# A PEER layer's dense expert products with 32 tokens taken out instead of 16, and GpSimd's share of the weight remainders laid out anew

## The reference, cut to what matters

```python
PEER_HEADS, PEER_NKEYS, PEER_TOPK = 8, 128, 16

def peer_ffn(h, w_pq, sub_keys, expert_u, expert_v):
    q = (h @ w_pq).reshape(B, S, PEER_HEADS, 2, PEER_DQ // 2)
    scores = jnp.einsum('bshpd,hpkd->bshpk', q, sub_keys)
    top_s, top_i = lax.top_k(scores, K)
    cand_s = top_s[..., 0, :, None] + top_s[..., 1, None, :]
    cand_i = top_i[..., 0, :, None] * NK + top_i[..., 1, None, :]
    best_s, best_pos = lax.top_k(cand_s.reshape(B, S, PEER_HEADS, K * K), K)
    expert_idx = jnp.take_along_axis(cand_i.reshape(B, S, PEER_HEADS, K * K), best_pos, axis=-1)
    gate = jax.nn.softmax(best_s, axis=-1)
    u = jnp.take(expert_u, expert_idx, axis=0)
    a = jnp.einsum('cd,chkd->chk', h, u)
    w = gate * jax.nn.gelu(a, approximate=False)
    return jnp.einsum('chk,chkd->cd', w, jnp.take(expert_v, expert_idx, axis=0))
```

## Time and profile before

| | |
|---|---|
| median of 3 runs | 2774.8 us (2772.82 to 2775.05) |
| profiled execution, its own time | 2772.15 us |
| its span, first to last instruction | 2770.4 us |
| PE busy | 2693.1 us, 97% of the span |
| DVE busy | 2127.9 us, 77% |
| ACT busy | 1381.1 us, 50% |
| POOL busy | 382.7 us, 14% |
| HBM | 206 GB/s over the span |

### The profile page before, as it was taken

One profiled execution on the slowest core, in us unless ns is written; L12 is line 12 of the kernel. 1 busy time (PEld: TensorE's weight loads), 2 busy tenths in 40 slices (PEclk: granted clock), 3 DMA queues, 4 the chain that ended last, 5 costly groups with the idle time before them and its releaser, 6 DMA issues.

```text
span 2770.4 us, 39894 instructions
## 1 busy us (share of the span) xinstructions
PE 2693.1 (97%) x16254; PEld 2321.3 (84%) x16254; DVE 2127.9 (77%) x3176; ACT 1381.1 (50%) x1632; POOL 382.7 (14%) x294
## 2 busy tenths in 40 slices
PE   7999999999999999999999999999999999999998
PEld 6778888788888888998888888897889988788887
DVE  7787887775555579989978777646699989888776
ACT  4645446554455455554444344464555554434443
POOL 0210002000023001122102012040011222002121
PEclk8999999999999999999999999999999999999999
DMA  8757876466553355555456588644555655456785
GB/s 312 268 198 296 313 257 225 155 213 197 190 199 129 135 190 191 205 198 170 166 183 212 185 290 295 225 150 139 165 180 197 209 182 176 149 198 218 258 289 185
DMA packets 86470, 574.34 MB, mean 207 GB/s; under 512 B 9840, under 2 KB 10352, under 8 KB 23056
## 3 DMA queue, kind: packets, MB, share of 16 engines
q1 hardware_dynamic: 75888, 534.86, 55.1%
q0 software_dynamic: 10400, 36.93, 3.8%
HBM read 563.32 MB, written 8.44 MB: 206 GB/s over the span
## 4 chain that ended last, share of the span: by engine, by line
PE 84%; DVE 8%; ACT 3%; issue 3%; DMA 1%; POOL 1%; SPq 0%; POOLq 0%; DVEq 0%; ACTq 0%
PE banks L492 22%; PE banks L499 11%; PE banks L590 11%; PE banks L592 10%; PE banks L600 10%; DVE wlo L1610 3%; PE banks L564 2%; PE banks L566 2%; PE banks L575 2%; ACT whi L1095 2%; PE banks L1030 2%; PE banks L534 1%; PE banks L536 1%; PE banks L546 1%; PE banks L630 1%
## 5 line engine op out<-in xcount | busy, mean ns | idle before, releaser
L1095 ACT ACTIVATE whi<-raw 128x2048 fp32r<-128x2048 f32 x438 | 839.7, 1917 | 962.6 <-issue 761.7
L1610 DVE TENSOR_TENSOR wlo<-raw,whi 128x2048 fp32r<-128x2048 f32 x422 | 977.0, 2315 | 240.6 <-ACT whi L1095 239.8
L492 PE MATMUL banks<-ht,whi 128*128 128x480 f32 (+1 forms) x2848 | 675.1, 387 | 5.9 <-DVE big L1708 3.4
L492 PEld LDWEIGHTS banks<-ht,whi 128*128 128x128 f32 x2848 | 524.0, 190 | 88.9 <-issue 3.6
L590 PE MATMUL banks<-whi,ht 128*128 128x512 f32 x1152 | 454.5, 395 | 10.4 <-DVE ht L1698 10.4
L592 PE MATMUL banks<-whi,ht 128*128 128x512 f32 x1152 | 449.8, 390 | 0.0
L499 PEld LDWEIGHTS banks<-ht,wlo 128*128 128x128 f32 x2848 | 351.7, 190 | 11.4
L499 PE MATMUL banks<-ht,wlo 128*128 128x240 f32 (+1 forms) x2848 | 354.0, 277 | 0.0
L600 PE MATMUL banks<-wlo,ht 128*128 128x512 f32 x1152 | 288.8, 390 | 2.1 <-DVE wlo L1610 2.1
L590 PEld LDWEIGHTS banks<-whi,ht 128*128 128x128 f32 x1152 | 216.9, 188 | 56.5 <-issue 12.1
L600 PEld LDWEIGHTS banks<-wlo,ht 128*128 128x128 f32 x1152 | 216.7, 188 | 47.9 <-DVE wlo L1610 3.0
(11 more groups left out here) (311 smaller groups left out, 3579.1 us busy)
## 6 DMA issues: line engine op xcount, KB each, us to landing
raw<-in_pu SPq DMA_DIRECT2D x128, 1024.0 KB, 4.9
raw<-in_pv SPq DMA_DIRECT2D x128, 1024.0 KB, 4.9
raw<-in_win SPq DMA_DIRECT2D x52, 1024.0 KB, 4.9
big<-in_wmod SPq DMA_DIRECT2D x28, 1024.0 KB, 7.1
raw<-in_wgate SPq DMA_DIRECT2D x22, 1024.0 KB, 6.4
raw<-in_wup SPq DMA_DIRECT2D x22, 1024.0 KB, 5.7
raw<-in_wdown SPq DMA_DIRECT2D x22, 1024.0 KB, 5.0
raw<-in_wmod SPq DMA_DIRECT2D x20, 1024.0 KB, 5.1
```

Of the source, the lines that this page charges most:

```text
L492: m = e.matmul(wide(b + n, t), h[:, q, c[n]], x[:, q], start=q == 0, stop=False, skip_group_check=True)
L1095: e.activation(whi(j), slot[u][0], ACT.Copy).then_inc(*hi.mark(j))
L1610: e.tensor_tensor(wlo(j), slot[u][0], whi(j).bitcast(F32), ALU.subtract).then_inc(*lo.mark(j))
```

## The change

Thirty-two tokens are left out instead of sixteen (NT 224, 28 groups, SUB 4, 32 dots and 32 additions a layer). In the first product POOL makes the remainders of 13 units (37, 39, ... 61) instead of 8, in the second those of 14 (1, 3, 5 and 10, 12, ... 30) instead of none. The list for the first has an entry for each head of the selection; all but the last are empty here. `pace` makes sets in odd units alone, two each and three in units 37, 49 and 61. The dots stand in units 9 to 34 and the additions in 37 to 61. The buffers of the tokens left out are laid out anew, two of the four row buffers, `HREP` and `ACC` behind the experts' results, and POOL's order in the second product is written unit by unit.

```diff
-FEW = 16
+FEW = 32
 NT = 256 - FEW
 SUB = P // FEW
 NG = NT // 8
 RINGS = 4
-POOLED = (37, 40, 43, 46, 49, 52, 55, 58)
+POOLED = (), (), (), (), (), (), (), (), tuple(range(37, 62, 2))
+POOLED_V = (1, 3, 5, *range(10, 31, 2))
...
-    OH = [[at(f"oh0{i}", 73728 + 4 * (29696 + 1024 * i), 2048, F16) for i in range(3)],
+    OH = [[at(f"oh0{i}", 73728 + 4 * (28672 + 1024 * i), 2048, F16) for i in range(3)],
...
-    HREP, ACC, ROWS_OF, PICK = 2048, 3072, 4096, 4096 + 1024 * RINGS
+    HREP, ACC, PICK = 28672, 29696, 2048
+    ROWS_OF = 30720, 31744, 2560, 3584
...
-    DENSE = -(-(IDC + FEW) // (2 * NT)) - 1
+    DENSE, DENSE_ROWS = -(-ROWS_OF[2] // (2 * NT)) - 1, -(-(ROWS_OF[3] + 1024) // (2 * NT)) - 1
...
-    pooled = {first["pu", l] + u for l in range(DEPTH) for u in POOLED}
+    pooled = {first["pu", l] + u for l in range(DEPTH) for us in POOLED for u in us}
+    pooled |= {first["pv", l] + v for l in range(DEPTH) for v in POOLED_V}
...
     def pace(u):
-        return 2 if u % 16 == 1 else 1
+        return 3 if u % 12 == 1 else 2 if u % 2 else 0
...
     def dots_due(v):
-        return 1 if 31 <= v < 47 else 0
+        return 0 if not 9 <= v < 35 else 2 if v % 4 == 2 and v < 34 else 1
 
     def adds_due(v):
-        return 0 if v < 48 or v > 60 else 2 if v % 4 == 1 else 1
+        return 0 if v < 37 or v > 61 else 2 if v % 4 == 1 else 1
...
-        if u >= 61:
+        if u >= 63:
...
-                if v == 48:
+                if v == 36:
                     on.wait_ge(*few.at((l, "dot", FEW - 1)))
...
         def gathered(l, m):
             r, n = m % RINGS, m % FEW
+            if m in (2, 3):
+                on.wait_ge(*part_lo.at(("w", l, DENSE_ROWS)))
...
+                if h < 7:
+                    for u in POOLED[h]:
+                        remainder(first["pu", l] + u)
...
-            for u in POOLED:
...
+            for u in POOLED[8]:
+                remainder(first["pu", l] + u)
...
-            on.wait_ge(*part_lo.at(("w", l, DENSE)))
-            ids(l)
-            for m in range(2 * FEW):
-                gathered(l, m)
+            asked = 0
+            for v in range(64):
+                if v + 1 in POOLED_V:
+                    remainder(first["pv", l] + v + 1)
+                if v == DENSE:
+                    on.wait_ge(*part_lo.at(("w", l, DENSE)))
+                    ids(l)
+                    gathered(l, 0)
+                    gathered(l, 1)
+                if v == DENSE_ROWS:
+                    gathered(l, 2)
+                    gathered(l, 3)
+                    asked = RINGS
+                if v >= DENSE_ROWS:
+                    while asked < min(2 * FEW, RINGS + sum(dots_due(x) + adds_due(x) for x in range(v + 1))):
+                        gathered(l, asked)
+                        asked += 1
```

More of the change, by code:

```diff
@@ L1041, in peer @@
                         m.then_inc(*turned.mark(("top", l, t)))
-                if u == 61:
+                if u == 63:
                     while plan.left():
@@ L1045, in peer @@
                             gate(0, g)
-                due = plan.step(pace(u))[0] if GATES < u < 61 else []
+                due = plan.step(pace(u))[0] if GATES < u < 63 else []
                 def between():
@@ L2317, in peer @@
                     slots_turned(l, 1)
-                if GATES < u < 61:
+                if GATES < u < 63:
                     gate_step(l, 0, *plan.step(pace(u)))
@@ L2329, in row @@
                 on.wait_ge(*d_row[r].at((l, m)))
-                return ag(ROWS_OF + 1024 * r, 1024)
+                return ag(ROWS_OF[r], 1024)
             def dot(n):
@@ L2603, in ids, with remainder @@
             e.tensor_tensor(ag(HREP, 1024), ag(HREP, 1024), ag(ACC, 1024), ALU.mult).then_inc(*p_rep.mark(l))
+        def remainder(j):
+            on.wait_ge(*hi.at(j))
+            on.wait_ge(*unit.at(j - NSP))
+            e.tensor_tensor(wlo(j), slot[place_of[j]][0], whi(j).bitcast(F32), ALU.subtract).then_inc(*p_lo.mark(j))
         def gathered(l, m):
             r, n = m % RINGS, m % FEW
+            if m in (2, 3):
+                on.wait_ge(*part_lo.at(("w", l, DENSE_ROWS)))
             if m >= RINGS:
@@ L2611, in gathered @@
             on.wait_ge(*p_ids.at((l, "v")))
-            e.indirect_dma_start(ag(ROWS_OF + 1024 * r, 1024), None, table,
+            e.indirect_dma_start(ag(ROWS_OF[r], 1024), None, table,
                                  bass.IndirectOffsetOnAxis(ag(at_ + n, 1).bitcast(U32), 0)).then_inc(*d_row[r].mark((l, m)))
```

## The result

The changed kernel takes 2797.2 us (median of 4 runs, 2788.9 to 2801.37) against 2773.99 for the kernel before beside it: 1.008 times as long, 95% interval 1.0056 to 1.0104. The profiled execution took 2788.9 us with a span of 2786.8.

What follows compares the result with a forecast made beforehand. PE was busy in 97% of the span, so a shorter PE stream pays only where nothing else is late. Selection -7, gate stage +51, second product +26: +70 a layer, +140 on 2772.15, 2912 us, median 2915; range 2815 to 2975.

Steps and rivals of the forecast that it cites:

- The columns: First product: 32 fewer columns save 0.22 us a unit in high matmuls, nothing in low ones; a unit goes 5.27 to 5.05.
- The selection: First product, units 0 to 33, where DVE sets 5.09 us a unit; with units 34 to 36 and 63, -7 us a layer.
- PE alone in the gate stage: First product, units 37 to 62: shorter matmuls, two gates fewer and no late row of gates give -16 us a layer.
- the burst: Last gates made in a row before unit 61 of the first product; forecast to go, 9 of the 16 us saved.
- The pairs 10 to 27 of the second product: Nine pairs of units with sets, dots and a POOL remainder overfill the shared port: 2.8 us each, 25 us a layer.
- the 15.5 end of my sum: Port time of such a pair, 14.3 us, or 15.5 if the products don't fall beside POOL; PE wants 11.97.
- POOL asks at +5.5, inside B's second operation, gets the port at +5.85: Gate stage, times from an odd unit's start: POOL's remainder blocks set B until +10.45, so PE waits 3.9 us, twelve times.
- the three-set units: Gate stage, at units 38 and 50, where three sets are made: 1.6 us more of PE waiting at each.
- 17 us of clock: Gate stage: PE's lowered clock behind each stall, 1.4 us per gap (ends 0 and 2.3), 17 us a layer.
- rival 2: Only the pairs of the second product stall, not the gate stage: +3 us a layer, 2781 us; chance 0.07.
- units 0 to 8: Second product: POOL's remainders for units 1, 3, 5 leave about 0.5 us of blocking at 3 and at 5, 1 us.
- rival 1: Sets end before POOL asks (later than +6.1 of the odd unit); if dots too leave the port free, 2731 us; chance 0.13.
- set B: The second of two one-hot sets DVE makes in an odd unit, ending at +6.4 undisturbed; PE wants it mid even unit.

Runs made afterwards that it cites:

- e1: The changed kernel with no remainder of the second product on POOL (GpSimd): 2735.8 us, 0.9877 of the kernel before.
- e8: The changed kernel with POOL's second-product remainders in every unit 10 to 30 instead of every second: 2845.7 us, 1.026 of the kernel before.
- e9: The changed kernel with POOL's second-product remainders replaced by a power of 28 elements behind the same waits: 2738.7 us, 0.9885 of the kernel before.
- e10: The changed kernel with the third operation of each one-hot set waiting for the end of the second: 2930.7 us, 1.0558 of the kernel before.

## Why the prediction was wrong

**Right.** The columns: high matmuls went to 0.204 us, low ones stayed at 0.112, a unit is 5.05. The selection, -7.0 for -7. PE alone in the gate stage, -16.3 for -16, with the burst and its lowered clock gone. The pairs 10 to 27 of the second product: 15.04 us each for the forecast 14.8 (11.95 before). The weighings don't fall beside POOL, since they queue behind a blocked dot or split. In e1 DVE fills such a pair, 12.45 us; less 2.28, plus 4.59 make 14.8. So it is the 15.5 end of my sum that happened, with DVE's work, 10.9 in my sum, 0.7 too high (12.45 - 2.28 is 10.2). Its form, an exclusive port taken in the dots by two SBUF inputs, is shown by e1, e8 and e9. The Trainium skill (GPSIMD Engine Reference, Key points) names such instructions as contending, and the dot at 6.10 us (1454.02 in the kernel after) agrees.

**Wrong.** The step "POOL asks at +5.5, inside B's second operation, gets the port at +5.85". The ask was right and the grant was not: POOL got it behind the set's last operation. With it fell 12 x 3.9 us of stalls, 3 us at the three-set units and 17 us of clock, 67 of the +70 a layer: the stage moved by -16.3 us for +51. What happened is rival 2, "only the pairs stall" (2781 us, 0.07), plus 5.1 us in units 0 to 8 for 1 and 26.9 in units 9 to 28 for 24. The sizes behind the step were sound: where e10 makes the grant come true, the stage costs 65.5 us for my 67: 44 us of stalls for 50 and 21.4 of clock for 17, two misses that partly cancel. The median is then 2930.7 for my 2915.

**Small misreadings, without effect.** 161.40 us with 1089 matmuls, 80 to a pair, makes 11.86 and not 11.97 (the units' starts give 11.95); the earlier trace rows gives 1.3 us for two splits and not 1.15; and before the change DVE's sets were blocked seven times a layer and not eight, since the remainder of unit 37 met none.

What misled me is the earlier trace rows: one case in which POOL got in between two of DVE's operations, behind an operation of its own. In the earlier trace rows and the other 13 cases in the gate stage before, POOL asked while DVE was idle or in a weighing, which reads PSUM and ran on beside it; that says nothing on who wins inside a stream. I took one sight for a rule, and gave rival 1, whose first half is what happened, a condition on time only (POOL asking later), where the true one was whether DVE leaves a gap.

**Units 0 to 8.** I looked at set B for units 3 and 5 only, and took unit 1 as free. POOL's remainder for unit 1 blocks the first one-hot operation of the second half (L2254 at 1381.31) for 4.13 us, in front of gates that PE wants at once. PE waits 3.6 us and runs unit 1 partly at 1.2 GHz (granted clock 0.77 in it): unit 0 takes 10.57 us for the 6.84 of e1, unit 1 7.10 for 5.57. Unit 3's remainder blocks a split for 4.67 us and costs nothing, and unit 5's waits the set out.

**The median** moved by 23 us where the profiled spans moved by 16; the profiled execution is the fastest of the four.

**Open.** What decides between the two engines when both ask at the end of an operation. The 166 to 2 count, the 24 of 24 and unit 4 fit "the holder keeps it while its next operation is ready in time"; the two exceptions and the earlier trace rows need something finer. In units 11 to 29 of the second product POOL gets in although DVE is full, and there its gather ends 0.02 us before its remainder starts. That POOL holds the port from the gather on would explain it, by the same rule, but isn't shown: at unit 29 the dot that started 0.91 us before the remainder was not blocked. Away from a gather and inside a gapless stream there is only unit 4, where POOL waited; a remainder moved there in units 9 to 28 wasn't tried.

## What to carry to other kernels

A remainder given to GpSimd is no relief for VectorE when it takes longer there (4.6 us) than on VectorE (2.3) and both need the same port: here it cost the difference wherever VectorE was full, and gained nothing where it had slack. Slack doesn't make it free either: if what it blocks is an operation that TensorE wants at once, the stall is paid whole (5.2 us in units 0 to 8, 65 in e10's gate stage). Before counting on or fearing a collision inside a stream, look whether the stream has gaps; a single added wait of 0.1 us turned a harmless overlap into 65 us a layer. With the remainders back on VectorE and the dots spread evenly, the rest of the change makes this kernel 1.8% faster.

## What the runs showed of the hardware that I had not expected

- A GpSimd operation that asks inside VectorE's gapless stream waits the whole stream out (up to 2.7 us: 7.3 for 4.61), and the stream isn't slowed; it was so for 166 of 168 in the gate stage.
- A GpSimd operation that computes for 4.8 us on 28 elements leaves VectorE's operations at their length, but for the dot behind the remainder that it waited for (1.26 for 1.21), while it can itself be held off by VectorE's (6.0 to 10.6 us in e9).
- A stall of 3.7 us costs PE half as much again (1.8 us in e10) by the granted clock behind it; behind the burst's gaps in the earlier trace rows it was 2.3 and 1.4.
